# GLA state products of two heads in one, key copies ahead of gate sigmoids, and mixed tiles cast on ScalarE

## The reference

```
h = h + 0.5 * swiglu(rms_norm(h), w1, w3, w2)
s5_in, q, k, v, r, a_low, g_s5, g_gla = split(rms_norm(h) @ w_in)
y_s5  = s5_mixer(s5_in, ...)
y_gla = gla_mixer(q, k, v, r, a_low, ...)
merged = sigmoid(g_s5) * (y_s5 @ proj_s5) + sigmoid(g_gla) * (y_gla @ proj_gla)
h = h + merged @ w_out

# gla_mixer: 4 heads, key width 64, value width 128, 8 chunks of 64 positions
bcum = cumsum(log_a) within the chunk
q_t, k_t = q * exp(bcum), k * exp(-bcum)
o_intra = tril(q_t k_t^T) v
k_end   = k * exp(b_last - bcum)
state_n+1 = exp(b_last) * state_n + k_end^T v
o_inter = q_t state_n
o = rms_norm_per_head(o_intra + o_inter) * g_norm * silu(r)
```

## Time and profile before

| | |
|---|---|
| three runs | 1882.17, 1883.85, 1885.89 us; median 1883.85 |
| the profiled execution | 1883.64 us, its span 1881.9 us |
| granted TensorE clock, mean | 0.996 |
| TensorE busy | 1855.5 us (99%) |
| VectorE busy | 1243.5 us (66%) |
| ScalarE busy | 523.6 us (28%) |
| GLA's units 10 to 14 | about 529 to 601 us of the span |
| merge of mixer 1 and start of `wout` | about 664 to 692 us |

### The profile page before, as it was taken

One profiled execution on the slowest core, in us unless ns is written; L12 is line 12 of the kernel. 1 busy time (PEld: TensorE's weight loads), 2 busy tenths in 40 slices (PEclk: granted clock), 3 DMA queues, 4 the chain that ended last, 5 costly groups with the idle time before them and its releaser, 6 DMA issues.

```text
span 1881.9 us, 21566 instructions
## 1 busy us (share of the span) xinstructions
PE 1855.5 (99%) x8620; PEld 1482.7 (79%) x8620; DVE 1243.5 (66%) x1670; ACT 523.6 (28%) x481; POOL 15.4 (1%) x57
## 2 busy tenths in 40 slices
PE   8999999999999999999999999999999999999997
PEld 6888888878888778888888888877778888788875
DVE  6763667667745487443244779979975788726874
ACT  5333222122322222221122112148852122212210
POOL 0000000000000000000000000000000000000000
PEclk9999999999999999999999999999999999999998
DMA  5224341472111332222322224232224222232221
GB/s 203 89 82 153 111 157 64 149 263 99 68 68 46 112 134 76 103 84 84 122 90 72 84 90 157 90 112 85 76 70 162 90 90 98 75 104 103 81 72 71
DMA packets 48132, 194.64 MB, mean 103 GB/s; under 512 B 6720, under 2 KB 15296, under 8 KB 33344
## 3 DMA queue, kind: packets, MB, share of 16 engines
q1 hardware_dynamic: 48064, 193.70, 29.9%
HBM read 180.84 MB, written 12.85 MB: 103 GB/s over the span
## 4 chain that ended last, share of the span: by engine, by line
PE 77%; issue 20%; DVE 3%; DMA 0%; ACT 0%; POOLq 0%; POOL 0%; SPq 0%; DVEq 0%
PE bank L942 23%; PE bank L943 23%; PE bank L944 23%; PE xb L1217 2%; DVE wlo L1292 1%; PE xb L1163 0%; PE xb L1153 0%; PE bank L1059 0%; PE bank L1060 0%; PE bank L1061 0%; PE xb L1171 0%; PE xb L981 0%; PE xb L1120 0%; PE xb L974 0%; DVE x L1336 0%
## 5 line engine op out<-in xcount | busy, mean ns | idle before, releaser
L942 PE MATMUL bank<-uhi,whi 128*128 128x512 f32 x1552 | 622.9, 401 | 7.2 <-DVE wlo L2138 7.0
L943 PE MATMUL bank<-ulo,whi 128*128 128x512 f32 x1552 | 616.7, 397 | 0.0
L944 PE MATMUL bank<-uhi,wlo 128*128 128x512 f32 x1552 | 616.6, 397 | 0.0
L654 ACT ACTIVATE whi<-raw 128x2048 fp32r<-128x2048 f32 (+3 forms) x177 | 299.9, 1694 | 1101.8 <-PE bank L944 1073.1
L1292 DVE TENSOR_TENSOR wlo<-raw,whi 128x2048 fp32r<-128x2048 f32 (+3 forms) x177 | 356.5, 2014 | 80.3 <-ACT whi L654 77.9
L942 PEld LDWEIGHTS bank<-uhi,whi 128*128 128x128 f32 x1552 | 293.3, 189 | 80.2 <-issue 9.7
L944 PEld LDWEIGHTS bank<-uhi,wlo 128*128 128x128 f32 x1552 | 293.3, 189 | 71.6
L943 PEld LDWEIGHTS bank<-ulo,whi 128*128 128x128 f32 x1552 | 293.6, 189 | 71.0 <-issue 1.4
L942 PE MATMUL bank<-hhi,whi 128*128 128x512 f32 x528 | 209.8, 397 | 2.3 <-DVE hlo L1345 1.2
L943 PE MATMUL bank<-hlo,whi 128*128 128x512 f32 x528 | 209.3, 396 | 0.0
L944 PE MATMUL bank<-hhi,wlo 128*128 128x512 f32 x528 | 209.3, 396 | 0.0
(11 more groups left out here) (391 smaller groups left out, 1815.4 us busy)
## 6 DMA issues: line engine op xcount, KB each, us to landing
raw<-in_up SPq DMA_DIRECT2D x65, 1024.0 KB, 4.8
raw<-in_win SPq DMA_DIRECT2D x16, 1024.0 KB, 4.8
raw<-in_wout SPq DMA_DIRECT2D x8, 1024.0 KB, 4.9
raw<-in_down1a SPq DMA_DIRECT2D x8, 768.0 KB, 4.4
tab<-tab_kept SPq DMA_DIRECT2D x4, 1536.0 KB, 8.6
raw<-in_down2a SPq DMA_DIRECT2D x8, 768.0 KB, 4.4
raw<-in_down3a SPq DMA_DIRECT2D x8, 768.0 KB, 4.3
raw<-in_down1b SPq DMA_DIRECT2D x8, 640.0 KB, 4.0
```

The source lines that it names most:

```text
L654: act.activation(whi[s][:, 0:width], raw[s][:, 0:width], ACT.Copy).then_inc(w_hi, 1)
L942: pe.matmul(dst, wh, hi, start=first, stop=False)
L943: pe.matmul(dst, wh, lo, start=False, stop=False)
L944: return pe.matmul(dst, wl, hi, start=False, stop=last)
```

## The change

Three edits. First, `q_f` and `eq` become the two halves of one tensor `q_heads`, and `outputs` makes the state products of both heads of a group and one chunk in one instruction: the moving operand is the chunk's 64 columns of `q_f` and of `eq`, the destination the two heads' columns of that chunk. The four value products now come first, and only the first of them carries `start`. Second, `keep_kend` is put first in ScalarE's jobs of unit 11, ahead of `sigmoids(1)`. Third, `merge` works on a unit of two tiles, in place in `gate_s`: both multiplies, the bank freed, the low half of the weight tile of unit i + 2 (for the last unit, behind everything), both adds, then, when ScalarE has cast each (`high_mix`, in ScalarE's list behind the cast of weight tile 24 + u), both subtractions.

```diff
-        eq = put("eq", [P, 2, S], at=at_kb(4))
-        q_f = put("q_f", [P, 2, S], at=at_kb(8))
+        q_heads = put("q_heads", [P, 2, 2, S], at=at_kb(4))
+        q_f, eq = q_heads[:, 0, :, :], q_heads[:, 1, :, :]
...
+                def high_mix(u):
+                    for m in range(2 * u, 2 * u + 2):
+                        act.wait_ge(mix_sum, m + 1)
+                        act.activation(mix_hi_1[:, m, :], gate_s[:, m, :], ACT.Copy).then_inc(mix_high, 1)
...
-                jobs[PAIR_FIRST + 1].append(keep_kend)
+                jobs[PAIR_FIRST + 1].insert(0, keep_kend)
...
+                for u in range(4):
+                    jobs.setdefault(M1["ps5"] + u + 2, []).append(lambda u=u: high_mix(u))
...
+                    o = XB[3].rearrange("p (h q) -> p h q", h=4)
                     for h in range(4):
-                        g, rows = head(h)
-                        pe.matmul(XB[3][:, h * P:(h + 1) * P], v_t[:, p, h * DV:(h + 1) * DV],
-                                  s_t[:, p % 2, h, :], start=True, stop=False)
+                        pe.matmul(o[:, h, :], v_t[:, p, h * DV:(h + 1) * DV], s_t[:, p % 2, h, :],
+                                  start=h == 0, stop=False)
+                    for g in range(2):
                         for c in range(2):
-                            at = h * P + c * CHUNK
                             tok = slice(p * P + c * CHUNK, p * P + (c + 1) * CHUNK)
-                            last = pe.matmul(XB[3][:, at:at + CHUNK], st[:, g, 2 * p + c, :],
-                                             q_of(h)[:, g, tok], start=False, stop=c == 1)
+                            last = pe.matmul(o[:, 2 * g:2 * g + 2, c * CHUNK:(c + 1) * CHUNK],
+                                             st[:, g, 2 * p + c, :], q_heads[:, :, g, tok],
+                                             start=False, stop=g == c == 1)
...
-                def merge(i, m, a, b):
-
+                def merge(u):
+
+                    i, m = M1["ps5"] + u, 2 * u
                     done(i)
                     for n in range(2):
-                        ins = tt(out=sq[:, :], in0=bank_of(i, n), in1=a[:, m + n, :], op=ALU.mult)
-                        if n:
-                            freed(i, ins)
-                        else:
-                            then(ins)
-                        then(tt(out=sq[:, :], in0=sq[:, :], in1=b[:, m + n, :], op=ALU.add))
-                        then(dve.tensor_copy(mix_hi_1[:, m + n, :], sq[:, :]))
-                        tt(out=mix_lo_1[:, m + n, :], in0=sq[:, :], in1=mix_hi_1[:, m + n, :].bitcast(F32),
-                           op=ALU.subtract).then_inc(mixed, 1)
-                        dve.wait_ge(mixed, m + n + 1)
+                        ins = tt(out=gate_s[:, m + n, :], in0=bank_of(i, n), in1=gate_s[:, m + n, :], op=ALU.mult)
+                    ins.then_inc(evac[(nb + i) % 2], 1)
+                    dve.wait_ge(evac[(nb + i) % 2], (nb + i) // 2 + 1)
+                    if u < 3:
+                        low(nb + i + 2)
+                    for n in range(2):
+                        tt(out=gate_s[:, m + n, :], in0=gate_s[:, m + n, :], in1=gate_g[:, m + n, :],
+                           op=ALU.add).then_inc(mix_sum, 1)
+                    for n in range(2):
+                        dve.wait_ge(mix_high, m + n + 1)
+                        tt(out=mix_lo_1[:, m + n, :], in0=gate_s[:, m + n, :],
+                           in1=mix_hi_1[:, m + n, :].bitcast(F32), op=ALU.subtract).then_inc(mixed, 1)
+                    if u == 3:
+                        low(nb + i + 2)
```

More of the change, by code:

```diff
@@ L412, in build @@
         mixed = sem("mixed")
+        mix_sum = sem("mix_sum")
+        mix_high = sem("mix_high")
         def pool_banks(nb):
@@ L2119, in mixer1 @@
                 for u in range(4):
-                    merge(M1["ps5"] + u, 2 * u, gate_s, gate_g)
+                    merge(u)
                 then(dve.memset(acc[:, :], 0.0))
```

## The result

Five runs of the changed kernel lie between 1876.30 and 1877.69 us, median **1876.83**; the kernel before has a median of 1883.85. The ratio is 0.9963, with a 95% interval of 0.9952 to 0.9973: 0.37% faster, 7.0 us. The forecast was 1876.8. The profiled execution took 1876.3 us, span 1874.5, at the same granted clock, 0.996.

What follows compares the result with a forecast made beforehand. TensorE, busy 99% (1855.5 of 1881.9 us), was taken as the bound. Savings of 3.57 + 1.58 + 1.98 - 0.1 = 7.0 us from the median 1883.85 gave a forecast of 1876.8 us, range 1874.2 to 1879.6.

Steps and rivals of the forecast that it cites:

- Output products: Mixer outputs on TensorE: eight records fewer per pair at 0.111 us each, 3.57 us saved over four pairs.
- The small term behind it: ScalarE's copy and square after the outputs: wider last record signals 0 to 0.1 us x 4 later, 0.1 taken in all.
- upper bound of part 1: Wide state products in the outputs: at most 0.234 us a record, adding 3.9 us, so a loss of 0.4.
- Key copies: First pair's state products on TensorE: wait for ScalarE's copies goes once these precede the sigmoids, 1.58 us saved.
- Merge: Mixer 1 into the output projection: TensorE's waits for VectorE's low half of a weight tile go, 1.86 plus 0.12, 1.98 us.
- 5.3, now under 5.62: VectorE's time per two-tile merge unit with casts on ScalarE, against TensorE's 5.62 us, so no lag builds up.
- Scan of states: VectorE's scan before the second pair's first output weight load: only 0.07 us left, said to move with the whole, costing nothing.
- Nothing given back after the mixer: TensorE after the mixer: no wait until the last norm, so the gain is kept.
- Busy time less 3.6, waits less 3.4: Sign of being right, on TensorE: busy time falls by about 3.6 us and its waits by 3.4.
- columns count: Rival on the outputs: wide products take as long as the two they replace, saving 3.5 us in all, 1880.3; chance 0.06.
- two-run form: Rival on the new state products: two distant runs make 32 records far dearer, 0.5 us each, 1889.3; chance 0.02.
- the moved wait: Rival before the output projection: VectorE waits for ScalarE's casts and TensorE still waits, 5.1 us saved, 1878.7; chance 0.10.

Runs made afterwards that it cites:

- half-column run: Changed kernel with state products taking only the even head's 64 columns, the odd head's share left out, equally many instructions: 1877.22 us, ratio 0.9965 to the kernel before.
- old merge: Changed kernel with the former merge of mixer 1 put back and ScalarE's casts taken out: 1879.06 us, ratio 0.9971 to the kernel before.
- scores in one: Changed kernel with the score products of two heads in one, 2 of 2x128 columns a pair instead of 4 of 128: 1876.53 us, ratio 0.9963 to before.
- low half last: Changed kernel, ScalarE's casts kept, with the weight tile's low half behind the subtractions in every unit: 1878.56 us, ratio 0.9968 to the kernel before.
- old key order: Changed kernel with ScalarE's key copies behind the sigmoids again: 1878.35 us, ratio 0.9971 to the kernel before.

## Why the prediction was right

- **Output products, 3.57 us less 0.1:** measured 3.41 by undoing it, and 4 x 0.88 = 3.5 in the outputs' stretches themselves (3.13 or 3.14 to 2.25). The step that carried it, that a record costs the same up to 128 columns, was confirmed by the half-column run; that the weight load is what it pays for stays an inference. The rule of the isolated spacing in the Trainium skill ("TensorE: Matmul & The Clock Gate", "Back-to-back issue gap"), by which narrow records would have been cheaper, doesn't describe this stream. By the rule in the Trainium skill, same page, section "LDWEIGHTS (loading the stationary operand)", a load of 128 columns takes, as an estimate, 107 ns; measured are 0.111 us a record. The small term behind it, up to 0.1 us each and 0.1 taken in all, was 0.14 to 0.16.
- **The upper bound of part 1 was wrong, without harm:** the 0.234 us that I took as the far value for a wider record is the pitch of fp32r products. The new state products are plain float32, of which a 512-column record takes 0.43 us. By that bound the part could have added 32 x 0.32 = 10 us, and not 3.9. Nothing of it came, since 128 columns cost 0.111.
- **Key copies, 1.58 us:** measured 1.59. The sigmoids were not delayed, and VectorE's scan started 0.1 us behind the products (537.38).
- **Merge, 1.98 us:** measured 1.96. The low half ended 1.05 us ahead of TensorE where I had 1.2, and a unit takes VectorE 5.14 us where I had 5.3. The account, a lag of 0.8 us a unit that adds up, is what the trace with the old merge shows. Which part of the edit removes the lag I had not asked: doing the like operations of two tiles without waits between them brings VectorE to TensorE's pace by itself, and the move of the casts to ScalarE, which the sum "5.3, now under 5.62" leans on, adds only spare time.
- **Scan of states, 0.07 us of margin:** held; in the second pair it ends at 555.19 + 1.25 = 556.44 and the first output weight load starts at 556.51.
- **Nothing given back after the mixer:** the part behind the stretch is 1198.9 us before and 1198.8 after.
- **Busy time less 3.6, waits less 3.4:** measured 3.8 and, in the waits view, 3.3 - 0.3 = 3.0; the view counts idle time alone.
- **The rivals:** columns count (1880.3) and two-run form (1889.3) were excluded by the same half-column run; the moved wait (1878.7) didn't come.

Part of the agreement is luck: the sum was right to 0.1 us, but in the ten traces the part before the stretch varied by 1.6 us (528.7 to 530.2) and that behind it by 3.0 (1197.4 to 1200.4). The traces show what makes up most of the second: TensorE's granted clock.

Between 1100 and 1118 us of the span it is 0.91 in five traces (before, old merge, half columns, scores in one, low half last) and 1.00 in the others; between 1804 and 1818 us it is 0.88 in four (changed, old key order, old merge, low half last) and 1.00 in the others. Each is a short fall from 2.4 to 1.2 GHz (in the kernel before products of 512 columns start at 1112.05, 1112.48 and 1112.90 us, 0.42 apart instead of 0.234), the first shortly after the single-column sums of a norm (16 products from 1108.36 us in the kernel before), the second shortly after a wait of TensorE for VectorE of 1.2 us. The part behind the stretch is 1197.4 to 1197.8 us with neither fall, 1198.8 to 1198.9 with one, and 1200.4 with both, so a fall costs some 1 to 1.5 us. The traces before and after have one each, and that they match is the luck.

The runs go with it as far as their clocks are listed: of the old merge's ten, the four fastest have a mean of 0.996 or 0.997, the four slowest 0.995. Why the clock falls in one execution and not in another with the same products was not tried and stays open, and so does part of what varies before the stretch.

## What to carry to other kernels

On an engine that is busy 99% of the time, count records and their pitch, start to start, rather than their durations, and ask of each whether it sits on the floor that all narrow records share or on the streaming of its columns; here merging products paid below 128 columns and not above. Price a wait as the stretch across it less the same stretch where nothing waits. When VectorE serves TensorE, check two things apart: that its whole unit fits in TensorE's, since a small excess adds up from unit to unit, and that what TensorE needs next (the bank, the low half of the next weight tile) goes out early enough in the unit. Leave out waits between operations that don't depend on each other: that alone made 5.62 us out of 6.42. To tell differences of 1 us in a kernel of 1880, compare a stretch between two fixed products in the traces, and look at the granted clock outside it.

## What the runs showed of the hardware that I had not expected

A plain float32 record in a 128x128 tile has a pitch of 0.111 to 0.113 us at 1, 64 and 128 columns alike, 0.215 at 256 and 0.43 at 512. Half of 0.215 is 0.108, so by this estimate the floor and the streaming of columns meet near 128 columns. Two independent casts of 128x512 on VectorE take 0.76 us together, where in the old chain one lasts 0.43 and the next operation starts 0.46 after it; two additions or multiplications of that size take 1.29 together and start 0.73 apart in the chain. The width of the last record of a group, 128 in place of 64 columns, delays the reader of its bank by 0.04 us. The mean granted clock of 0.995 to 0.997 hides up to two short falls to 1.2 GHz inside the kernel, which cost some 1 to 1.5 us each.
